# Score steps without GpSimd and every fourth row of the second expert table summed on VectorE, in a two-layer hybrid decoder trunk

## What is computed

```python
# mixer: scores inside a chunk, for each of the feature groups
b = jnp.cumsum(gc, axis=2)
diff = b[:, :, :, None, :] - b[:, :, None, :, :]
decay = jnp.where(causal, jnp.exp(jnp.where(causal, diff, 0.0)), 0.0)
scores = jnp.sum(qc[:, :, :, None, :] * kc[:, :, None, :, :] * decay, axis=-1)

# PEER: 8 heads x 16 experts per token, out of 16384, each a row of 1024 in two tables
act = jax.nn.gelu(jnp.einsum('thkd,td->thk', u_tab[ec], xc), approximate=False)
return jnp.einsum('thk,thkd->td', gc * act, v_tab[ec])

# then
x = layer_norm(ALPHA * x + peer_ffn(x, ...))
```

## Time and profile before

| | |
|---|---|
| median of 3 runs | 4024.07 us |
| the profiled execution | 4012.16 us |
| its span, first to last instruction | 4010.3 us |
| TensorE (PE) busy | 3506.6 us, 87% |
| VectorE (DVE) busy | 2547.5 us, 64% |
| GpSimd (POOL) busy | 2536.0 us, 63% |
| ScalarE (ACT) busy | 1024.9 us, 26% |
| read from HBM | 1259.74 MB, 316 GB/s over the span |

### The profile page before, as it was taken

The page is one execution under the profiler, slowest core; times in us unless marked ns, Lnnn a source line. Parts: engine busy times, 40 slices in busy tenths (PEclk is TensorE's granted clock), DMA queues, the critical chain, the costliest instruction groups (busy, mean ns, idle before and its releaser), DMA issues. The chain is left out here.

```text
span 4010.3 us, 42088 instructions
## 1 busy us (share of the span) xinstructions
PE 3506.6 (87%) x13480; PEld 2009.5 (50%) x13480; DVE 2547.5 (64%) x6604; ACT 1024.9 (26%) x2150; POOL 2536.0 (63%) x2420
## 2 busy tenths in 40 slices
PE   8797698999999799898899799999999968786878
PEld 7576364555555365344566256446555524332434
DVE  2636877666367986667556985567636788845442
ACT  2321122333122223222312222223312223212211
POOL 0312557887675655878765654688757677777773
PEclk9788799999999999999999999999999999999999
DMA  5025898889999999888999988888989999999996
GB/s 185 23 84 200 288 333 302 315 322 348 339 357 376 329 344 341 309 318 307 353 347 374 371 293 317 286 327 317 335 327 352 371 356 386 402 376 355 373 396 231
DMA packets 331050, 1270.02 MB, mean 317 GB/s; under 512 B 38336, under 2 KB 39616, under 8 KB 313808
## 3 DMA queue, kind: packets, MB, share of 16 engines
q0 software_dynamic: 299520, 1090.65, 73.9%
q1 hardware_dynamic: 31312, 176.67, 11.5%
HBM read 1259.74 MB, written 7.44 MB: 316 GB/s over the span
## 5 line engine op out<-in xcount | busy, mean ns | idle before, releaser
L822 PE MATMUL Y<-GV,DIAG 128*128 128x512 f32 x4096 | 1985.2, 623 | 294.7 <-DMA GV<-in_vtab,IDX 246.9
L1041 POOL DMA_INDIRECT GV<-in_vtab,IDX x1024 | 1157.9, 1131 | 612.8 <-PE Y L822 389.4
L1763 DVE SCALAR_TENSOR_TENSOR GU<-GU,X 128x1024 f32<-128x1024 f32 x1024 | 1237.2, 1226 | 475.7 <-DMA GU<-in_utab,IDX 473.4
L1041 POOL DMA_INDIRECT GU<-in_utab,IDX x1024 | 1149.2, 1122 | 585.5 <-issue 265.6
L822 PEld LDWEIGHTS Y<-GV,DIAG 128*128 128x128 f32 x4096 | 767.0, 196 | 1256.0 <-issue 982.9
L517 PE MATMUL A<-XT,WR 128*128 128x264 f32 (+1 forms) x2496 | 581.0, 388 | 18.7 <-ACT R L1255 10.5
L517 PEld LDWEIGHTS A<-XT,WR 128*128 128x128 f32 x2496 | 482.0, 194 | 146.8 <-issue 76.0
L1288 ACT ACTIVATE DIAG<-C,WGT 128x128 f32<-128x128 f32 x1024 | 372.2, 392 | 714.7 <-PE Y L822 589.0
L977 POOL TENSOR_TENSOR R<-R 128x256 f32<-128x256 f32 (+3 forms) x256 | 127.1, 529 | 149.5 <-DVE R L1440 88.8
L736 PE MATMUL D<-WR,R 96*128 96x256 f32 (+3 forms) x800 | 190.3, 395 | 15.8 <-POOL R L995 15.8
L736 PEld LDWEIGHTS D<-WR,R 96*128 96x128 f32 (+3 forms) x800 | 142.2, 179 | 71.9 <-POOL R L995 17.7
(11 more groups left out here) (216 smaller groups left out, 2932.4 us busy)
## 6 DMA issues: line engine op xcount, KB each, us to landing
WR<-in_wstream SPq DMA_DIRECT2D x96, 1024.0 KB, 7.7
WR<-in_wstream SPq DMA_DIRECT2D x36, 1280.0 KB, 9.2
GU<-in_utab,IDX POOLq DMA_INDIRECT x1024, 6.5
GV<-in_vtab,IDX POOLq DMA_INDIRECT x1024, 6.5
R<-in_lnp SPq DMA_DIRECT2D x14, 512.0 KB, 7.0
SS<-in_st_in SPq DMA_DIRECT2D x12, 384.0 KB, 6.2
out_st_s<-SS SPq DMA_DIRECT2D x12, 384.0 KB, 6.9
WR<-in_wstream SPq DMA_DIRECT2D x16, 256.0 KB, 6.1
```

Of the source, the lines that this page charges most:

```text
L822: last = nc.tensor.matmul(Y[0:rows, c], scaled, GV[:, v % RV, c], start=(j == 0), stop=(j == end - 1))
L1041: pool.indirect_dma_start(ring[:, i % places, :], None, table, bass.IndirectOffsetOnAxis(ap=idx, axis=0)).then_inc(fetched[i % places], 16)
L1763: nc.vector.scalar_tensor_tensor(out=u, in0=u, scalar=1.0, in1=X[:, tile_of(g), :], op0=ALU.mult, op1=ALU.mult, accum_out=SCORE[:, g % 2, ...
```

## The change

1. **Rows of V on VectorE.** Of the rows j = 4 to 126 of a group, those with j % 4 == 2 in the first six groups, and in the last 24 rows of all those with odd j, are no longer multiplied by TensorE (186 and 11 rows). No diagonal is made for them. VectorE adds WGT times the row to a new sum YS in SBUF (`add_row`, one tick after TensorE would have had the row). ScalarE starts YS as ALPHA * X at the group's beginning (`begin_sum`), and at the end VectorE adds YS and Y. The gather into a place that VectorE frees waits for v_added, not v_used, and stands one tick later in GpSimd's program, ahead of the tick's U gather.
2. **Score steps.** GpSimd has no part in them. VectorE makes the differences of the four tokens in one instruction, after waiting for p_used itself; the mask is one instruction over only the 4 x 4 block at the diagonal; each product is one instruction.
3. SG and SCS are moved into the large region R, over parts of S, to make room for YS.

```diff
+def by_vector(v):
+    kind, _, j = ROWS[v]
+    if kind == "s" or not 4 <= j < SLOTS - 1:
+        return False
+    return j % 4 == 2 if v < STEP_AT[3] else v >= TAIL and j % 2 == 1
...
             def accumulate(v):
                 kind, g, j = ROWS[v]
+                if VEC[v]:
+                    return
...
-                yield "rot", s, 3
-                pool.wait_ge(sems["b_ready"], s + 1)
-                differences(0)
-                differences(1)
...
             def fetch_v(i):
-                if i >= RV:
-                    pool.wait_ge(sems["v_used"], i - RV + 1)
+                if i >= RV and VEC[i - RV]:
+                    pool.wait_ge(sems["v_added"], VEC_NO[i - RV])
+                elif i >= RV:
+                    pool.wait_ge(sems["v_used"], PE_NO[i - RV])
                 fetch(GV, vtab, v_fetched, RV, i)
...
+                if 0 <= t - 1 + RV - LAG < NROW and late(t - 1 + RV - LAG):
+                    fetch_v(t - 1 + RV - LAG)
                 if 0 <= t + RU < NROW:
                     fetch_u(t + RU)
-                if 0 <= t + RV - LAG < NROW:
+                if 0 <= t + RV - LAG < NROW and not late(t + RV - LAG):
                     fetch_v(t + RV - LAG)
...
+            def begin_sum(t):
...
+                if kind == "b" and j == 0 and g in SHARED:
+                    if v:
+                        act.wait_ge(sems["y_read"], groups_before(v))
+                    nc.scalar.activation(YS[:, :], X[:, tile_of(g), :], ACT.Copy, scale=ALPHA) \
+                        .then_inc(sems["sum_begun"], 1)
...
                 def low(step):
-                    iq = quarter(step)[1]
-                    wd = 4 * iq + 4
-                    dve.wait_ge(sems["diff_ready"], 16 * s + step + 1)
+                    f, iq = quarter(step)
+                    at, wd = 4 * iq, 4 * iq + 4
+                    if step >= 2:
+                        dve.wait_ge(sems["p_used"], 16 * s + step - 1)
+                    dve.drain()
+                    b = Z[:, f, 0:HP]
+                    nc.vector.tensor_tensor(P[:, step % 2, :, :, 0:wd], each(b, at, wd), among(b, wd), ALU.subtract)
+                    dve.drain()
                     m = const("causal").rearrange("p (i j) -> p i j", j=CH)
-                    for i in range(4):
-                        p = P[:, step % 2, i, :, 0:wd]
-                        last = nc.vector.tensor_tensor(
-                            p, p, m[:, 4 * iq + i:4 * iq + i + 1, 0:wd].to_broadcast([128, NC, wd]), ALU.min)
+                    p = P[:, step % 2, :, :, at:wd]
+                    last = nc.vector.tensor_tensor(
+                        p, p, m[:, at:wd, at:wd].unsqueeze(2).to_broadcast([128, 4, NC, 4]), ALU.min)
                     last.then_inc(sems["min_ready"], 1)
...
-                    for i in range(4):
-                        p = P[:, step % 2, i, :, 0:wd]
-                        nc.vector.tensor_tensor(p, p, kk[:, :, 0:wd], ALU.mult)
+                    p = P[:, step % 2, :, :, 0:wd]
+                    nc.vector.tensor_tensor(p, p, among(Z[:, 4 + f, 0:HP], wd), ALU.mult)
                     dve.drain()
...
+                    last = nc.vector.tensor_tensor(p, p, each(Z[:, 8 + f, 0:HP], 4 * iq, wd), ALU.mult)
                     last.then_inc(sems["p_ready"], 1)
...
+            def add_row(v):
+
+                _, g, j = ROWS[v]
+                dve.wait_ge(sems["sum_begun"], SHARED.index(g) + 1)
+                dve.wait_ge(v_fetched[v % RV], 16 * (v // RV + 1))
+                dve.drain()
+                nc.vector.scalar_tensor_tensor(out=YS[:, :], in0=GV[:, v % RV, :], scalar=WGT[:, g % 2, j:j + 1],
+                                               in1=YS[:, :], op0=ALU.mult, op1=ALU.add).then_inc(sems["v_added"], 1)
+
             def add_experts(v):
...
+                if kind == "b" and g in SHARED:
+                    dve.drain()
+                    nc.vector.tensor_tensor(x, YS[:, :], Y[:, :], ALU.add).then_inc(sems["y_read"], 1)
+                    return
...
             for t in range(NTICK):
+                if t > LAG and VEC[t - LAG - 1]:
+                    add_row(t - LAG - 1)
                 if t < NROW:
                     dot(t)
```

More of the change, by code:

```diff
@@ L80, with groups_before @@
 NTICK = NROW + LAG
+TAIL = NROW - LAG
+def by_vector(v):
[3 more added lines that the diff above has]
+    return j % 4 == 2 if v < STEP_AT[3] else v >= TAIL and j % 2 == 1
+VEC = [by_vector(v) for v in range(NROW)]
+VEC_NO = [sum(VEC[:v + 1]) for v in range(NROW)]
+PE_NO = [v + 1 - VEC_NO[v] for v in range(NROW)]
+DIAGONALS = [v for v in range(NROW) if ROWS[v][0] == "b" and not VEC[v]]
+DIAG_NO = {v: k for k, v in enumerate(DIAGONALS)}
+SHARED = sorted({ROWS[v][1] for v in range(NROW) if VEC[v]})
+def groups_before(v):
+    return len({r[:2] for r in ROWS[:v]})
 def tile_of(g):
@@ L310, in build @@
         DIAG = sb("DIAG", 128, NDIAG, 128)
+        YS = sb("YS", 128, D)
         R = sb("R", 128, 16272)
@@ L352, in build @@
         FIN = sb("FIN", 128, 2, 96)
-        SG = sb("SG", 128, 2, 256)
+        SG = view(12400, 2, 256)
+        SCS = view(12912, 2, 2 * NKEY)
         EQT = sb("EQT", 128, 2, TOPK, TOPK)
@@ L807, in accumulate @@
                 kind, g, j = ROWS[v]
[L808 to L811, removed]
+                if VEC[v]:
+                    return
+                if j == 0 and v:
+                    pe.wait_ge(sems["y_read"], groups_before(v))
                 if kind == "b":
-                    pe.wait_ge(sems["diag_ready"], v + 1 - sum(r[0] == "s" for r in ROWS[:v]))
-                    scaled, rows, end = DIAG[:, v % NDIAG, :], 128, SLOTS
+                    pe.wait_ge(sems["diag_ready"], DIAG_NO[v] + 1)
+                    scaled, rows, end = DIAG[:, DIAG_NO[v] % NDIAG, :], 128, SLOTS
                 else:
@@ L1014, in mixer @@
                         squares(hd)
[L1015 to L1018, removed]
                     for hd in heads_before(i):
@@ L1021, in mixer @@
                         gated(hd)
[L1022 to L1026, removed]
                 yield "t", s
@@ L1052, in fetch_u, with late @@
                 fetch(GU, utab, u_fetched, RU, i)
+            def late(i):
+                return i >= RV and VEC[i - RV]
             def fetch_v(i):
-                if i >= RV:
-                    pool.wait_ge(sems["v_used"], i - RV + 1)
+                if i >= RV and VEC[i - RV]:
+                    pool.wait_ge(sems["v_added"], VEC_NO[i - RV])
+                elif i >= RV:
+                    pool.wait_ge(sems["v_used"], PE_NO[i - RV])
                 fetch(GV, vtab, v_fetched, RV, i)
@@ L1281, in diagonal @@
                 kind, g, j = ROWS[v]
-                if kind == "s":
+                if v not in DIAG_NO:
                     return
@@ L1285, in diagonal @@
                     act.wait_ge(sems["w_ready"], PH * g + j // TOPK + 1)
-                if v >= NDIAG:
-                    act.wait_ge(sems["v_used"], v - NDIAG + 1)
-                nc.scalar.activation(DIAG[:, v % NDIAG, :], ident, ACT.Copy, scale=WGT[:, g % 2, j:j + 1]) \
+                k = DIAG_NO[v]
+                if k >= NDIAG:
+                    act.wait_ge(sems["v_used"], PE_NO[DIAGONALS[k - NDIAG]])
+                nc.scalar.activation(DIAG[:, k % NDIAG, :], ident, ACT.Copy, scale=WGT[:, g % 2, j:j + 1]) \
                     .then_inc(sems["diag_ready"], 1)
+            def begin_sum(t):
+                if t < LAG + 1 or t - LAG - 1 >= NROW:
+                    return
+                v = t - LAG - 1
+                kind, g, j = ROWS[v]
+                if kind == "b" and j == 0 and g in SHARED:
[3 more added lines that the diff above has]
+                        .then_inc(sems["sum_begun"], 1)
             def exps(t):
@@ L1331, in _ @@
                     diagonal(t + AHEAD - LAG)
+                begin_sum(t)
                 work.run(t)
```

40 lines of the change are left out of this document (10 added, 30 removed).

## The result

The changed kernel takes 3870.12 us (median, 3854.27 to 3882.36), the kernel before 4024.03 us: ratio 0.9614, 95% interval 0.9578 to 0.9651. It is faster by 154 us. Forecast were 84 us, 3940 us, with 3885 to 3975 us around it.

The account below looks back on a forecast made before the run. It took TensorE to bound most of the first part, DMA the second, TensorE the last. From the profiled 4012.2 us, -75 (first part) and -9 (tail) gave 3928, or 3940 us against the median of the runs; range 3885 to 3975.

Parts of the forecast that it names:

- Net on VectorE: nothing: Score steps: VectorE's time stays the same, 3.16 us per step before and 3.12 after, -3 us over 64 steps.
- I count nothing: Score steps: GpSimd gains 96 us of its own time in the first part, but waits 500 us there: 0.
- the handing over: First part, 450 to 3150 us: loss as the lead passes between engines, taken as 150 us after the change.
- More is gained: Rival: VectorE's and GpSimd's mutual waits held the rings; 75 us lost between engines, not 150: 3865 us, chance 0.14.
- sum of largest needs: First part: largest of TensorE, VectorE and byte needs per 50 us stretch, added up: 2567 us before, 2475 after.
- lost where the lead passes: First part: the real 2700 us lie 133 us above the summed needs, lost where one engine takes over from another.
- The moved rows: First part: 186 rows take 335 us off TensorE and add 233 us to VectorE; first part -75 us.
- The tail: Last 43 us: 11 rows go to VectorE, gathers are next, 34 us remain: -9 us; 3150 to 3933 us: 0.
- The first mixer: Before 400 us: the wait for a free half of P moves to VectorE; between 0 and 5 us, taken as 0.
- VectorE sets the pace: Rival: each added row on VectorE delays a dot and then GpSimd's next two gathers: 4060 us, chance 0.13.
- Held descriptors: Rival: each added row on VectorE holds one gather for 1.14 us, 212 us more for GpSimd: 4045 us, chance 0.03.
- The DMA caps it: Rival: at 376 GB/s, with 30 us more lost in handing over, the gain is 32 us: 3983 us, chance 0.11.

Follow-up runs that it names:

- experiment 1: Kernel before the change with the new score steps alone, no row moved to VectorE: 3930.53 us, ratio 0.9777.
- experiment 6: Kernel before, no row moved; GpSimd out of the score steps, VectorE doing differences, full-width mask and products in four instructions each: 3961.22 us, ratio 0.9846.
- experiment 2: Kernel before with the 197 rows moved to VectorE, score steps left as they were: 3971.25 us, ratio 0.9882.
- experiment 4: Changed kernel, but VectorE adds only 8 of 1024 columns of each moved row (output incomplete): 3811.3 us, ratio 0.9483.
- the open-ticks kernel: Changed kernel with no row moved in VectorE's full ticks, 167 rows in all: 3850.63 us, ratio 0.9589, beside the changed kernel's 3865.95 us.
- experiments 8: The open-ticks kernel with every third instead of every fourth row moved there, 205 in all: 3857.76 us, ratio 0.9603.
- experiment 9: The open-ticks kernel with every second instead of every fourth row moved there, 320 in all: 3889.09 us, ratio 0.9678.

## Why the prediction was right and where it was not

**The direction and the lead** were right: TensorE held the first part, VectorE had room for a quarter of the rows, and afterwards its share (78%), the DMA share (0.94, forecast above 0.93) and GpSimd's waits stand where the forecast put them. The size was not: 154 us where 84 were forecast. TensorE is at 88%, above the 80 to 85% forecast.

**The score steps** were the term that failed: "Net on VectorE: nothing", "I count nothing" for GpSimd, and VectorE's 93.6 us of waits put into the small change of the handing over. Measured: 86 us. The rival "More is gained" (3865 us, chance 0.14) is what came out, and it named the waits between VectorE and GpSimd. Two steps of the working are behind the miss. The first is the waits. In VectorE's program a wait for GpSimd is also a wait for what stands ahead in GpSimd's program, and that can be VectorE itself. The kernel before, VectorE and GpSimd in order of time, with the idle time before each in brackets:

```profile
620.68 0.08 DVE L1763 DVE_READ_ACCUMULATOR GU<-GU,X 128x1 f32 x1
626.54 2.88 DVE L1455 TENSOR_TENSOR R<-R,C 128x256 f32<-128x256 f32 x4 [5.78 <-POOL R L977]
629.35 1.21 DVE L1763 SCALAR_TENSOR_TENSOR GU<-GU,X 128x1024 f32<-128x1024 f32 x1
```
```profile
623.16 0.93 POOL L1041 DMA_INDIRECT GV<-in_vtab,IDX  x1 [1.19 <-PE Y L822]
624.11 4.36 POOL L977 TENSOR_TENSOR R<-R 128x256 f32<-128x256 f32 x8
630.84 0.95 POOL L1041 DMA_INDIRECT GU<-in_utab,IDX  x1 [2.37 <-DVE GU L1763]
```

VectorE ends a dot at 620.8 and stands 5.8 us for the differences. These stand in GpSimd's program behind a gather that waits for TensorE. Then VectorE masks, makes its next dot at 629.35, and only when that is done can GpSimd issue its next gather, at 630.84: no gather is issued from 624.1 to 630.8, a time in which at the usual two in 3.5 us nearly four would be. 4.4 us of it are GpSimd's own differences (of two steps, at a mixer's beginning), 2.4 the wait for VectorE. From 620 to 660 us the kernel before has a DMA share of 0.70 at 235 GB/s; the changed kernel in the same stretch 0.86 at 306, in which it is a few ticks further on:

```profile
620.00:660.00 40.00, 27.43 (x75) 11.33 (x74) 32.46 (x91) 8.05 (x19) 25.20 (x32) 0.87 0.70 235
```
```profile
620.00:660.00 40.00, 32.34 (x155) 16.63 (x156) 36.15 (x72) 8.39 (x21) 26.79 (x23) 0.91 0.86 306
```

A circle that closes on VectorE like this one is the smaller part, though. Read back in the same way, VectorE's 21 waits of the first part (93.6 us) fall on 43 us in which GpSimd issues gathers that stand ahead, 36 in which it writes the differences, 9 in which such a gather waits for TensorE, and 0.4 for VectorE. Behind the differences 10 gathers wait for VectorE, 28 us in all. GpSimd's own time on them, 103 us in this part, holds up every gather behind it as well. How the 38 to 57 us divide between that time and the waits was not tried apart.

The forecast's sum of largest needs can't see this, since it uses busy times: it lay in the 133 us "lost where the lead passes", and I took 150 for it afterwards. The same sum as an estimate from the other traces, with the same three needs in stretches of 50 us, has 61 us lost from 450 to 3000 us in experiment 1 and 73 in experiment 6, 152 in experiment 2, and 106 in the changed kernel. So 150 is right for moved rows with the old score steps. The step that failed is that the new ones were given too small a share in it: by this estimate they take 60 to 72 us of the 133 away.

The second step is VectorE's time. I took each old group at its shortest row, 1.42 us. The groups were longer on average, as here with 2.88 us while GpSimd worked beside it; the three old groups of all 64 steps are 226 us in the trace (1.18 us each, not 1.03), and the four new instructions 191 us in experiment 1, so that 35 us of busy time went, where the forecast's figures without drains give 13. The two further drains of each step, 0.08 us each, take 10 of that back, so some 25 us went, not 3. By the row of the single instruction nothing was wrong: 1.23 us for 1024 elements, 0.42 for the mask, as forecast. The four-dimensional pattern costs nothing:

```profile
603.50 1.23 DVE L1481 TENSOR_TENSOR R<-R 128x1024 f32<-128x1024 f32 x1
604.80 0.42 DVE L1486 TENSOR_TENSOR R<-R,C 128x256 f32<-128x256 f32 x1
608.25 1.21 DVE L1495 TENSOR_TENSOR R<-R 128x1024 f32<-128x1024 f32 x1
609.53 1.23 DVE L1497 TENSOR_TENSOR R<-R 128x1024 f32<-128x1024 f32 x1
```

The Trainium skill's price (VectorE: DVE Perf Modes, The TRN2 errata), with 35 us more for VectorE, would have come nearer, but not for the right reason: in undisturbed rows four merged instructions differ by 0.2 us, as forecast, not by its 0.47.

**The moved rows** came out smaller than forecast: -75 us in the first part were forecast; measured are 46 us alone and 66 to 68 on top of the score steps, the tail included. Taken apart, the forecast's sum (the same 54 stretches, needs and prices) gives 172 us for the relief alone, and for the load 40 us without the relief and 80 with it. Measured are 119 for the relief and 49 and 52 for the load. So the relief was sized too high, and so was the load beside it. The forecast took 355 us off TensorE; its busy time fell by 238 from experiment 1 to the changed kernel (3487.3 to 3249.1), since the remaining rows took longer (below). TensorE's longer wait for rows of V (164 us, 85 before) is no new wait for VectorE, which the forecast called free: it is as long in experiment 4, where VectorE adds next to nothing. The stretch from 450 to 3000 us of that run:

```profile
PE Y L849 <- DMA GV<-in_vtab,IDX: 168.2, 95, 7.4
```

The two errors have opposite signs: too little for the score steps (0 for 86), too much for the rows (84 for 66 to 68).

**The tail.** Behind the last dot TensorE's rows took 43 us before, 37 after (3797 to 3834); forecast were 34. As forecast, gathers are next: of TensorE's 9.7 us idle there 9.1 are for rows of V. GpSimd issues 20 gathers there in 28 us, where 18 in 25 were forecast, which is the 3 us; they came at 328 GB/s, not at the 380 assumed. From tick 768 to 1023, where hardly a row was moved, the changed kernel loses 8 us, the score steps alone 4, the open-ticks kernel none; forecast was 0. Some 8 of the change's rows still fell into VectorE's full ticks there (the forecast left them in the first part).

**The first mixer** shows a gain of 11 us in the profiled run of the changed kernel, 3 in experiment 1 and none in experiment 6; the forecast's 0 to 5 can't be told from what runs differ by.

**The rivals.** "VectorE sets the pace" is true in places: 8 to 10 us lost in each full stretch, and as a whole somewhere between 205 moved rows, which bring no more than 167, and 320, which lose 38 us (experiments 8 and 9). The changed kernel in its full stretch:

```profile
2210.00:2260.00 50.00, 33.05 (x84) 16.09 (x83) 45.88 (x114) 14.69 (x30) 24.13 (x23) 0.73 0.69 229
```

VectorE has 45.9 of 50 us, the gathers 229 GB/s. "Held descriptors": a gather's mean went from 1.12 and 1.13 us to 1.15; against experiment 4 the 2048 gathers are 47 us longer in all, 0.24 us for each added row, not 1.14. The Trainium skill's rule (SBUF — State Buffer, Who interferes with whom) agrees with this in kind, but the price is a fifth of what the full length of the 1.3 us instruction would give. That the shared port is the cause was not tried. "The DMA caps it": 349 GB/s in the first part with a share of 0.94, and 358 in experiment 4: so the changed kernel was not at the most that the DMA engines give.

## What to carry to other kernels

A compute instruction on the queue that also issues gathers is not hidden by that queue's waiting time. The engine that waits for it also waits for the gathers ahead of it, and the gathers behind it stand still while it runs. Here GpSimd waited 500 us for others in the first part, and taking the differences off it (127 us of its time, or 83 when merged) still brought 57 and 38 us. So read a wait back through the program of the engine that is waited for before pricing it as hidden, above all where the chain returns to the engine that waits. When an engine is relieved by another one, move work only in the stretches in which the helper has room; moving fewer rows (167 in place of 197) was faster.

## What was not expected of the hardware

**TensorE's remaining work became slower as it had less.** In the first part the granted clock was 0.97 in experiment 1, 0.92 in the changed kernel, 0.88 with every second row moved, and the mean of a Y matmul 617, 661 and 699 ns; the projections' mean hardly moved. In the stretch at 2210 us above, in which TensorE was idle for a third of the time, it stood at 0.73. By an estimate from that figure this is about half of the time at the lower of its two levels (1.2 and 2.4 GHz). The groups of the first part, of experiment 1, the changed kernel and experiment 9:

```profile
L849 PE MATMUL Y<-GV,DIAG 128*128 128x512 f32 x2856 | 1369.0, 617 | 113.0 <-DMA GV<-in_vtab,IDX 83.4 <-DVE X L1846 18.2 <-ACT DIAG L1291 10.9
L544 PE MATMUL A<-XT,WR 128*128 128x264 f32 (+1 forms) x1680 | 393.0, 388 | 4.0 <-issue 4.0
```
```profile
L849 PE MATMUL Y<-GV,DIAG 128*128 128x512 f32 x2204 | 1150.5, 661 | 201.0 <-DMA GV<-in_vtab,IDX 163.6 <-DVE X L1844 17.1 <-ACT DIAG L1291 14.3
L544 PE MATMUL A<-XT,WR 128*128 128x264 f32 (+1 forms) x1823 | 423.5, 387 | 7.4 <-issue 7.4
```
```profile
L852 PE MATMUL Y<-GV,DIAG 128*128 128x512 f32 x1723 | 973.3, 699 | 290.2 <-DMA GV<-in_vtab,IDX 240.7 <-ACT DIAG L1294 27.0 <-DVE X L1847 15.7
L547 PE MATMUL A<-XT,WR 128*128 128x264 f32 (+1 forms) x1760 | 421.8, 397 | 15.7 <-issue 15.7
```

How much of the lengthening is the clock and how much is a matmul's share of time in which it waits was not tried apart.

**A tensor_tensor on VectorE beside one on GpSimd** took twice its time: 2.88 us for the group of four at 626.54, where a group of the same size takes 1.42. Over all steps it is little: in experiment 6 the same mask instructions take 70 us in all without GpSimd beside them, 76 before.
